# Layer norms with the low parts of weights behind the centring, and a router that picks before its softmax

## The reference

```python
def layer_norm(x, g, b):
    mu = jnp.mean(xf, axis=-1, keepdims=True)
    var = jnp.mean(jnp.square(xf - mu), axis=-1, keepdims=True)
    return (xf - mu) * lax.rsqrt(var + LN_EPS) * g + b
...
    logits = (xt @ router).astype(jnp.float32)
    top_v, top_i = lax.top_k(logits, TOP_K)          # 2 of 8 experts
    w = jax.nn.softmax(top_v, axis=-1)
    for e in range(N_EXPERTS):
        y = y + combine[:, e:e + 1] * swiglu(xt, w_gu[e], w_down[e])
...
    # layer 3: x = layer_norm(ALPHA * x + pool_mixer(x)), then + swiglu(x), layer_norm
    # layer 4: x = layer_norm(ALPHA * x + nsa_mixer(x)),  then + moe_ffn(x), layer_norm
```

## Time and profile before

| | us |
|---|---|
| median of 3 runs | 2365.77 (2365.38 to 2366.56) |
| the profiled execution | 2364.67 |
| its span | 2362.7 |
| TensorE busy | 2306.9 (98%) |
| VectorE busy | 1883.2 (80%) |
| ScalarE busy | 1321.7 (56%) |

### The profile page before, as it was taken

One profiled execution on the slowest core, in us unless ns is written; L12 is line 12 of the kernel. 1 busy time (PEld: TensorE's weight loads), 2 busy tenths in 40 slices (PEclk: granted clock), 3 DMA queues, 4 the chain that ended last, 5 costly groups with the idle time before them and its releaser, 6 DMA issues.

```text
span 2362.7 us, 35947 instructions
## 1 busy us (share of the span) xinstructions
PE 2306.9 (98%) x14903; PEld 2076.6 (88%) x14903; DVE 1883.2 (80%) x2007; ACT 1321.7 (56%) x1293; POOL 2.4 (0%) x8
## 2 busy tenths in 40 slices
PE   9999999999999999999999899999999999999997
PEld 9799999989989998999997788888888888888886
DVE  6796887787968968555567678999898989898887
ACT  6544333554443334434336367767777777777775
POOL 0000000000000000000000000000000000000000
PEclk9999999999999999999999999999999999999999
DMA  6243444533434443545330289999999999999995
GB/s 259 101 169 136 167 179 179 183 130 116 164 134 167 180 179 125 209 179 183 121 124 11 89 317 374 368 348 360 360 374 363 343 359 375 360 344 358 373 359 209
DMA packets 169552, 556.76 MB, mean 236 GB/s; under 512 B 8752, under 2 KB 8880, under 8 KB 133168
## 3 DMA queue, kind: packets, MB, share of 16 engines
q1 hardware_dynamic: 168192, 547.45, 63.2%
q10 hardware_dynamic: 1008, 6.49, 0.7%
q0 software_dynamic: 192, 0.52, 0.1%
HBM read 552.86 MB, written 1.05 MB: 234 GB/s over the span
## 4 chain that ended last, share of the span: by engine, by line
PE 88%; DVE 6%; ACT 4%; issue 1%; DMA 0%; DVEq 0%; ACTq 0%; SPq 0%
PE ps L1057 14%; PE ps L1059 14%; PE ps L1058 13%; PE ps L1051 12%; PE ps L1053 12%; PE ps L1052 12%; PE ps L1216 2%; ACT whi L607 2%; DVE wlo L1845 1%; PE ps L1159 1%; PE ps L1469 1%; PE ps L1671 1%; PE ps L1297 1%; PE ps L1319 1%; PE ps L1238 1%
## 5 line engine op out<-in xcount | busy, mean ns | idle before, releaser
L1845 DVE TENSOR_TENSOR wlo<-raw,whi 128x2048 fp32r<-128x2048 f32 x519 | 1185.7, 2288 | 251.3 <-ACT whi L607 192.2
L607 ACT ACTIVATE whi<-raw 128x2048 fp32r<-128x2048 f32 x519 | 993.8, 1916 | 563.9 <-PE ps L1053 323.1
L1051 PE MATMUL ps<-hh,whi 128*128 128x256 f32 x1952 | 558.1, 286 | 11.5 <-DVE hl L1947 7.1
L1052 PE MATMUL ps<-hl,whi 128*128 128x256 f32 x1952 | 553.3, 283 | 0.0
L1053 PE MATMUL ps<-hh,wlo 128*128 128x256 f32 x1952 | 553.3, 283 | 0.0
L1051 PEld LDWEIGHTS ps<-hh,whi 128*128 128x128 f32 x1952 | 375.7, 192 | 14.2 <-DVE hl L1947 7.2
L1057 PE MATMUL ps<-whi,hh 128*128 128x512 f32 x960 | 386.0, 402 | 2.0 <-DVE hl L2707 2.0
L1059 PE MATMUL ps<-wlo,hh 128*128 128x512 f32 x960 | 377.5, 393 | 0.0
L1058 PE MATMUL ps<-whi,hl 128*128 128x512 f32 x960 | 376.5, 392 | 0.0
L1052 PEld LDWEIGHTS ps<-hl,whi 128*128 128x128 f32 x1952 | 375.8, 193 | 0.3
L1053 PEld LDWEIGHTS ps<-hh,wlo 128*128 128x128 f32 x1952 | 375.6, 192 | 0.0
(11 more groups left out here) (372 smaller groups left out, 2552.8 us busy)
## 6 DMA issues: line engine op xcount, KB each, us to landing
raw<-stream SPq DMA_DIRECT2D x519, 1024.0 KB, 5.4
work<-w_in ACTq DMA_DIRECT2D x1, 2240.0 KB, 10.3
stage<-stage_consts ACTq DMA_DIRECT2D x4, 512.0 KB, 4.0
work<-mem_in ACTq DMA_DIRECT2D x2, 1024.0 KB, 5.1
x<-x_in SPq DMA_DIRECT2D x1, 1024.0 KB, 4.9
out<-x SPq DMA_DIRECT2D x4, 256.0 KB, 2.3
const<-consts SPq DMA_DIRECT2D x1, 548.5 KB, 9.4
work<-work POOLq DMA_DIRECT2D x4, 128.0 KB, 3.1
```

What stands on the lines that cost most here:

```text
L607: nc.scalar.activation(whi[hi_at(g, odd)][:, :], raw[g % RAWS][:, :], ACT.Copy).then_inc(hi_ready, 1)
L1051: mm(out_ap, hi_w, hi_x, start=start, stop=False, **kw)
L1052: mm(out_ap, hi_w, lo_x, start=False, stop=False, **kw)
L1845: V.tensor_tensor(wlo[g % RAWS][:, :], raw[g % RAWS][:, :], whi[hi_at(g, odd)][:, :].bitcast(F32), ALU.subtract).then_inc(lo_ready[g % RAW ...
```

## The change

- Layer norms 0 to 2 take an argument `beside`: a `split_lo` that stood ahead of the layer norm (in LN1, ahead of the last additions of the FFN) is done between the centring and the wait for rstd.
- ScalarE no longer adds the bias in place and rounds then. It writes the rounded part with the bias directly (`with_bias` to `hh`), VectorE makes the low part with the bias in the same operation, and ScalarE adds the bias to `x` itself once the low part of that quarter is there. LN3 is unchanged in effect. Two later additions to x and the branch gates wait for `x_ready` in addition.
- In pool, VectorE folds quarters 0 to 2 of x between its additions, and LN0's mean uses the folded sums.
- The router multiplies x, as weights, with the router's 8 columns, so that the logits stand with tokens on partitions at once; the copy and the turn back go. The marks come from the two places directly, the weights of the experts are worked out later, in the branch. The tokens' split is done in two halves. The numbers of warming products are changed.

```diff
@@ -652,15 +651,23 @@
                 norm_act(8 + i, D, 1e-5)
-                for c in range(QUARTERS + 1):
-                    if c < QUARTERS:
-                        act.wait_ge(norm_scaled, QUARTERS * (SCALED_AT["ln"] + i) + c + 1)
-                        for b in (2 * c, 2 * c + 1):
-                            ins = nc.scalar.activation(xb(b), xb(b), ACT.Identity, bias=R("ln_b", 8 * i + b))
-                        ins.then_inc(x_ready, 1)
-                    if c and not last:
-                        act.wait_ge(x_ready, QUARTERS * i + c)
-                        round_quarter(c - 1, x)
+                def with_bias(c, to, done):
+                    for b in (2 * c, 2 * c + 1):
+                        ins = nc.scalar.activation(to[:, b * BLK:(b + 1) * BLK], xb(b), ACT.Identity, bias=R("ln_b", 8 * i + b))
+                    ins.then_inc(done, 1)
+                for c in range(QUARTERS):
+                    act.wait_ge(norm_scaled, QUARTERS * (SCALED_AT["ln"] + i) + c + 1)
+                    if last:
+                        with_bias(c, x, x_ready)
+                    else:
+                        with_bias(c, hh, hi_done)
+                if not last:
+                    for c in range(QUARTERS):
+                        act.wait_ge(h_ready, QUARTERS * (13 + i) + c + 1)
+                        with_bias(c, x, x_ready)
@@ -974,10 +981,11 @@
             layer_norm_act(2)
+            for tt in range(2):
+                act.wait_ge(x_turned, tt + 1)
+                nc.scalar.activation(FEW_TOK_HI[:, tt * 1024:(tt + 1) * 1024], banks(3 + 2 * tt), ACT.Copy).then_inc(x_tokens, 1)
...
             nc.scalar.activation(small[:, 504:506], small[:, 504:506], ACT.Exp).then_inc(top2_exp, 1)
-            act.wait_ge(x_turned, 1)
-            nc.scalar.activation(FEW_TOK_HI, banks(3, 4), ACT.Copy).then_inc(x_tokens, 1)
@@ -1526,15 +1534,15 @@
-            layer_norm_pe(0, lambda: sums_pe(x, MEAN_BANK[0], lambda c: pe.wait_ge(pool_added, c + 1) if c < 3 else pe.wait_ge(banks_drained, ph.e + 1))
-                          .then_inc(mean_ready, 1), 12)
+            layer_norm_pe(0, lambda: folded_mean_pe(0, 1, [(3, lambda: pe.wait_ge(banks_drained, PHASES["pool"].e + 1))]), 12)
             ffn_pe(2, 14, norm=8, idle=22)
-            layer_norm_pe(1, lambda: folded_mean_pe(1, 1, [(3, lambda: pe.wait_ge(acc_drained, QUARTERS * 3))]), 12)
+            layer_norm_pe(1, lambda: folded_mean_pe(1, 2, [(3, lambda: pe.wait_ge(acc_drained, QUARTERS * 3))]), 12)
...
                 pe.wait_ge(w1_loaded, 16)
+                pe.wait_ge(x_ready, QUARTERS * 2)
@@ -1631,26 +1639,22 @@
             proj_pe("nsa_out", 16)
-            layer_norm_pe(2, lambda: folded_mean_pe(2, 2, [(3, lambda: pe.wait_ge(banks_drained, PHASES["nsa_out"].e + 4))]), 12)
+            layer_norm_pe(2, lambda: folded_mean_pe(2, 3, [(3, lambda: pe.wait_ge(banks_drained, PHASES["nsa_out"].e + 4))]), 12)
             pe.wait_ge(rstd_ready, 11)
-            keep_warm(7, 24)
+            keep_warm(7, 14)
...
                     pe.wait_ge(x_ready, QUARTERS * 2 + b // 2 + 1)
-                mm(ps[0:8, 0, 0:BLK], R("router", b * 8, 8), xb(b), start=(b == 0), stop=(b == NB - 1)).then_inc(logits_t, 1)
-            keep_warm(7, 4)
-            pe.wait_ge(logits_kept, 1)
-            for tt in range(2):
-                last = nc.tensor.transpose(ps[:, 1, tt * 8:(tt + 1) * 8], W(50)[0:8, tt * P:(tt + 1) * P], ident[0:8, 0:8])
+                for tt in range(2):
+                    last = mm(ps[:, 1, tt * 8:(tt + 1) * 8], x[:, b * BLK + tt * P:b * BLK + (tt + 1) * P], R("router", b * 8, 8),
+                              start=b == 0 and tt == 0, stop=b == NB - 1, skip_group_check=True)
...
                     last = turn(ps[:, 3 + 2 * tt + c // 4, (c % 4) * P:(c % 4 + 1) * P], x[:, c * BLK + tt * P:c * BLK + (tt + 1) * P])
-            last.then_inc(x_turned, 1)
-            keep_warm(7, 14)
+                last.then_inc(x_turned, 1)
+            keep_warm(7, 2)
@@ -1658,7 +1662,7 @@
             last.then_inc(counts_ps, 1)
-            keep_warm(7, 14)
+            keep_warm(7, 16)
@@ -1980,7 +1985,7 @@
-            def layer_norm(i, g_at, last=False):
+            def layer_norm(i, g_at, last=False, beside=None):
@@ -1989,6 +1994,8 @@
                     ins.then_inc(ln_centred, 1)
+                if beside is not None:
+                    split_lo(beside)
@@ -1998,7 +2005,11 @@
                         dve.wait_ge(hi_done, QUARTERS * HI_AT[f"ln{i}"] + c - 1)
-                        low_quarter(c - 2, x)
+                        for b in (2 * c - 4, 2 * c - 3):
+                            cols = slice(b * BLK, (b + 1) * BLK)
+                            ins = V.scalar_tensor_tensor(out=hl[:, cols], in0=xb(b), scalar=R("ln_b", 8 * i + b), in1=hh[:, cols].bitcast(F32),
+                                                         op0=ALU.add, op1=ALU.subtract)
+                        ins.then_inc(h_ready, 1)
@@ -2076,7 +2087,8 @@
                         for s in range(ph.n):
-                            split_lo(ph.g + s + AHEAD)
+                            if conv or i < 3 or s < ph.n - 1:
+                                split_lo(ph.g + s + AHEAD)
@@ -2112,6 +2124,8 @@
                         split_act(s, f)
+                if not conv:
+                    dve.wait_ge(x_ready, QUARTERS)
@@ -2529,12 +2543,17 @@
                 ins.then_inc(pool_added if g < 3 else banks_drained, 1)
+                if g in (1, 2):
+                    dve.wait_ge(pool_added, g + 1)
+                if g == 1:
+                    link(fold_x(1))
+                if g == 2:
+                    fold_x(2).then_inc(x_folded, 1)
...
             dve.wait_ge(banks_drained, PHASES["pool"].e + 1)
-            split_lo(PHASES["pool"].g + AHEAD)
-            layer_norm(0, 0)
+            layer_norm(0, 0, beside=PHASES["pool"].g + AHEAD)
             conv_ffn(2, None, ALPHA)
-            layer_norm(1, 8)
+            layer_norm(1, 8, beside=PHASES["nsa_in"].g - 1 + AHEAD)
@@ -2643,12 +2662,10 @@
+            dve.wait_ge(x_ready, QUARTERS * 2)
             proj_add("nsa_out", ALPHA, then={1: lambda: nsa_fold(1), 2: lambda: nsa_fold(2)})
-            split_lo(FIRST + AHEAD)
-            layer_norm(2, 16, last=True)
-            dve.wait_ge(logits_t, NB)
-            V.tensor_copy(W(50)[0:8, :], ps[0:8, 0, 0:BLK]).then_inc(logits_kept, 1)
+            layer_norm(2, 16, last=True, beside=FIRST + AHEAD)
@@ -2656,29 +2673,46 @@
                 step(V.max_index(idx[:, 8 * tt:8 * tt + 8], small[:, 464 + 8 * tt:472 + 8 * tt], small[:, 448 + 8 * tt:456 + 8 * tt]))
-            sync()
-            step(V.tensor_copy(small[:, 480:496], idx[:, :]))
...
             sync()
-            dve.wait_ge(top2_exp, 1)
-            link(V.tensor_scalar(small[:, 506:508], small[:, 504:506], 1.0, None, ALU.add))
-            link(V.reciprocal(small[:, 506:508], small[:, 506:508]))
-            link(V.tensor_tensor(small[:, 508:510], small[:, 504:506], small[:, 506:508], ALU.mult))
+            link(V.tensor_copy(small[:, 480:496], idx[:, :]))
             for tt in range(2):
-                link(V.tensor_scalar(small[:, 576 + 8 * tt:584 + 8 * tt], C("iota8"), small[:, 480 + 8 * tt:481 + 8 * tt],
-                                     small[:, 506 + tt:507 + tt], ALU.is_equal, ALU.mult))
-                link(V.tensor_scalar(small[:, 592 + 8 * tt:600 + 8 * tt], C("iota8"), small[:, 481 + 8 * tt:482 + 8 * tt],
-                                     small[:, 508 + tt:509 + tt], ALU.is_equal, ALU.mult))
-            link(V.tensor_tensor(small[:, 576:592], small[:, 576:592], small[:, 592:608], ALU.add))
-            V.tensor_scalar(small[:, 608:624], small[:, 576:592], 0.0, None, ALU.is_gt).then_inc(picked, 1)
-            dve.wait_ge(x_tokens, 1)
-            V.tensor_tensor(FEW_TOK_LO, banks(3, 4), FEW_TOK_HI.bitcast(F32), ALU.subtract).then_inc(x_tokens_lo, 1)
+                step(V.tensor_scalar(small[:, 592 + 8 * tt:600 + 8 * tt], C("iota8"), small[:, 481 + 8 * tt:482 + 8 * tt], None, ALU.is_equal))
+            sync()
+            for tt in range(2):
+                ins = V.scalar_tensor_tensor(out=small[:, 608 + 8 * tt:616 + 8 * tt], in0=C("iota8"), scalar=small[:, 480 + 8 * tt:481 + 8 * tt],
+                                             in1=small[:, 592 + 8 * tt:600 + 8 * tt], op0=ALU.is_equal, op1=ALU.add)
+            ins.then_inc(picked, 1)
+            def tokens_low(tt):
+                cols = slice(tt * 1024, (tt + 1) * 1024)
+                dve.wait_ge(x_tokens, tt + 1)
+                V.tensor_tensor(FEW_TOK_LO[:, cols], banks(3 + 2 * tt), FEW_TOK_HI[:, cols].bitcast(F32), ALU.subtract).then_inc(x_tokens_lo, 1)
+            def expert_weights():
+                dve.wait_ge(top2_exp, 1)
...
+                V.tensor_tensor(small[:, 576:592], small[:, 576:592], small[:, 592:608], ALU.add).then_inc(routed, 1)
+            tokens_low(0)
...
```

(3 more changed lines are left out.)

23 lines of the change are left out of this document (17 added, 6 removed).

## The result

The changed kernel takes 2353.36 us (median of 5 runs, 2351.71 to 2354.95), the kernel before 2365.77 (5 runs beside them, 2365.38 to 2368.13): ratio 0.9948, 95% interval 0.9937 to 0.996, so faster by 12.4 us where 7.8 were forecast, and 0.1 us outside the low end of the range. (The 7.8 us lead to 2358.0 from the median and to 2356.9 from the profiled execution.) The profiled execution took 2353.4 (span 2351.5, mean granted clock 0.992) against 2364.67: 11.3 us. In the later sessions before took 2365 (84 more runs, 2360 to 2370), so the gain to explain is 11 to 12 us. Single runs of one kernel differ by 3 to 12 us, so a difference of a few us between two medians is weak evidence by itself.

A forecast was written before the change was run, and what follows sets the result against it. TensorE, holding 88% of the chain of waits, was taken to bound the kernel. Norms 6.5 plus router 1.3 made 7.8 us off 2364.67: 2356.9, or 2358.0 against the median; range 2353.5 to 2362.3.

The forecast's parts named there:

- The norms: Layer norms after pool, dense FFN and attention output: earlier centring and first products gain 1.6, 2.5 and 2.4, together 6.5 us.
- ScalarE's second pass over x: In LN0, ScalarE's eight bias operations on x itself end about 1 us later; nothing was taken for it.
- the branch gates' new wait: In LN1, TensorE waits for all of x behind its second slot; ScalarE was expected done several us before.
- rival 3: Norms: moved low parts or ScalarE's second pass delay rstd or first products; half of 6.5 gone, 2361.3 us; chance 0.12.
- The router: Between rstd and first slot: 4.0 us gained at full clock; 1.3 with the expected low clock, bounds 5.8 and -3.
- Logits and flag: Router, counted from TensorE's start behind rstd: logits at T+5.6, flag at T+9.6, or T+11.6 at the low clock.
- The picks: Router: VectorE's picking with 13 of 18 small instructions takes 2.2 to 2.75 us, 2.4 taken, ready at T+8.0.
- the row of 15 columns: Profile row: the clock fell during 64 records of 15 columns; the 8-column logits were expected to do likewise.
- rival 1: Router: the clock stays full through the logits; 2355.3 us, down to 2353.5; chance 0.22.
- the price of that low clock: Router: slow transposes 1.5, counts 0.7, warming products 0.6, together 2.8 us until the gather, plus 0.8 in it.
- Rival 2: Router: the clock stays low through the gather and two slots' worth of products; 2362.3 us, less of it 2359.5; chance 0.18.

The follow-up runs named there:

- the combined version: Changed kernel plus 11 instead of 16 warming products, one-column products in groups of four, 36 zero products in the last wait: 2351.86 us, again 2350.26.

## Why the prediction was right or wrong

**The norms: right, term by term.** 1.5, 2.4 and 2.3 us in the trace against 1.6, 2.5 and 2.4; in LN1 the low part is 1.9 of it and the rounding with the bias 0.6 (forecast 2.0 and 0.5). No price appeared for ScalarE's second pass over x or the branch gates' new wait; rival 3 is out.

**The router: the places right, the clock's price too high.** Logits and flag came where they were forecast. The picks took 1.9 us, less than the 2.2 that the prediction took as the least, and were 0.4 early. The clock fell behind the logits in twelve of the thirteen profiled executions with the new router (four times for 3.4 us, seven times for 6.8, once for 10.2), as the row of 15 columns had suggested and rival 1 denied; between rstd and the gather of the old router it fell in none of five.

**The step that failed** is the price of that low clock in the router's sum: 2.8 us until the gather and 0.8 in the gather. The one execution with the clock full started the gather at T+11.2, and the changed kernel's with its fall of 6.8 us at T+13.4, so the price until the gather was 2.2. The transposes lost 0.7 where 1.5 was put down, for the clock fell only 1 us after they began (and 16 times 0.12, doubled, would have been 1.9); the counts lost 0.7 as forecast, and the gather, which waited for the places when the clock was full, now had to wait 0.8 longer for the warming products (forecast 0.6). The price in the gather was nothing: it ran at the full clock in both executions of the changed kernel. After falls of 3.4 us the gather started at T+12.5, after the others of 6.8 at up to T+14.2, and after 10.2 at T+15.1. Where the forecast's sum has 4.0 - 2.8 - 0.8 = 0.4 us until the first slot, the trace has 2.4: 1.4 by the two prices, the rest mostly by the picks, since with the clock full the gather came 0.5 earlier than forecast. Another 1.6 us (0.9 was given back in the forecast, for the first slot) came by the seventh slot. But the norms alone gained the same 1.6 there, so it is not shown to be the router's. Taken alone, the router's part gave nothing that a measurement can tell (0.9993, 0.9984 to 1.0002, with its program moved).

**A second step failed,** one that the sum took without saying so: that outside of the router the clock would be as in the one trace of before. In the two profiled executions the rest is there. Up to pool's end the changed kernel lost 1.14 us (2.1 in and behind a fall at 595 us that before had not, 0.7 won back at a shorter one at 926); between LN1 and LN2, where the clock fell in before and not in it, it won 3.05; behind the seventh slot it lost 0.84, of which 0.3 is the wait behind the branch. With the norms and the router (2.4 and the 1.6, less rounding 3.97) the sum is -1.14 + 1.51 + 2.43 + 3.05 + 2.29 + 3.97 - 0.84 = 11.27, the difference of the two profiled executions. Of the 3.5 us beyond the forecast's 7.8, 2.7 are in the router's term, 1.1 outside of it, and the norms fell 0.3 short.

Where exactly the time came to lie is in part luck: the same program, profiled again, ended 3.2 us earlier by other falls, and the median lies 0.1 us outside of a range whose low end was worked out for a clock that stays full, which it did not.

That the time agrees with rival 1 (2355.3, down to 2353.5) is no point for it: the clock did fall behind the logits. One execution of the combined version had what rival 1 says, the clock full through the transposes, so it is rare and not excluded. Rival 2 did not come: the gather ran at the full clock in both executions of the changed kernel, and the first slot had one fall of 3.4 us.

What stays open: whether the change makes the fall at the 15-column products rarer. In twelve profiled executions with the norms' part of the change (the shifted ones and the one with the old rounding among them) it was missing in seven, lasted 3.4 us in two and 6.8 in three; with the low parts ahead of the centring again it lasted 3.4; in four with the norms of before it came each time, once for 3.4 and else for 6.8 us. One and the same program up to this place had none in two executions of the changed kernel and 6.8 us in three of kernels that were edited behind it only (the combined version twice, and the same without the zeros at the end). Shifts in time of 1.7 and 3.4 us did not bring it back. No experiment held the clock up there; the zeros between the products made it worse.

**What no step had:** the wait behind the experts' branch. In before it is zero, in the changed kernel 0.3 to 0.6 us, and in the parts taken alone 2.4 and 2.9. With it the parts gave 4.6 and -1.9 us, with their programs moved by a few products 8.9 and 1.1, which comes to 10.0 against the 11 to 12 of the whole. The two shifted kernels, with 14 and 28 products more on the way there, had no such wait. The changed kernel with eight products more at the start, in a wait, measured 2.6 to 3.6 us more than without them: had the change left TensorE's program at another length, the same edits could have measured a gain that much smaller.

## What to carry to other kernels

Work out a moved instruction from the rows at its place: the norms' terms came out to 0.1 us here. But before the sum is set against a median, ask in which places the one trace shows a low granted clock, and widen the range by what each fall costs, since the same program has them in one execution and not in the next. A fall slows only what runs during it: ask when it begins, and which of the slowed products anything waits for. And when one part of a change is timed alone, look for idle time without a releaser behind a branch: shift the program by a few hidden instructions before the part is blamed.
